# A mixer and expert block: x transposed raw, its norm applied to the transposed tiles

## The reference, cut to what matters

```python
h = x * rsqrt(mean(x*x, axis=-1) + 1e-6) * attn_norm_w        # the first norm
proj = h @ w_in                                                # 1024 -> 2568
qkv, z, beta_logit, a_in, p = split(proj)
qkv = silu(causal_depthwise_conv(qkv, conv_w))                 # 4 taps
o = chunk_gated_delta_rule(q, k, v, g(a_in), sigmoid(beta_logit))
x = x + concat([norm(o) * silu(z), multiscale_pool(p)]) @ w_out
x = x + moe(norm(x), ...)                                      # top 4 of 32, 402 MB of weights
return norm(x)
```

## Time and profile before

| | us |
|---|---|
| three runs | 1407.25, 1410.95, 1411.27 |
| median | 1410.95 |
| the profiled execution, its own time | 1406.2 |
| its span in the trace | 1404.5 |
| TensorE busy in the span | 1280.6 |
| ScalarE, VectorE, GpSimd busy | 293.3, 497.9, 159.2 |

### The profile page before, as it was taken

How to read it: one execution, slowest core, us unless ns; L and a number is a source line. 1 busy time by engine, 2 the same in 40 slices (tenths; PEclk the granted TensorE clock), 3 DMA queues, 4 the chain that set the end, 5 groups by cost and what they waited for, 6 DMA issues and landing times.

```text
span 1404.5 us, 53101 instructions
## 1 busy us (share of the span) xinstructions
PE 1280.6 (91%) x22067; PEld 754.5 (54%) x22067; DVE 497.9 (35%) x1614; ACT 293.3 (21%) x504; POOL 159.2 (11%) x256
## 2 busy tenths in 40 slices
PE   5999999993799999999999999999999999988860
PEld 3456655442455555555555656555555565555430
DVE  4453023215333333333333333333333333332227
ACT  4432212204111112112211121111211111211102
POOL 3100240007010010101100010101101010100000
PEclk9999999995899999999999999999999999999995
DMA  6222132308289999999999999999999999999957
GB/s 207 78 60 62 32 120 76 132 18 335 105 335 416 408 415 402 416 410 418 402 414 403 399 416 400 416 408 417 405 410 411 404 417 399 418 419 417 417 204 295
DMA packets 94582, 447.32 MB, mean 318 GB/s; under 512 B 10973, under 2 KB 22706, under 8 KB 61194
## 3 DMA queue, kind: packets, MB, share of 16 engines
q1 hardware_dynamic: 90778, 437.34, 77.4%
q0 software_dynamic: 3696, 8.40, 1.6%
HBM read 432.52 MB, written 14.88 MB: 319 GB/s over the span
## 4 chain that ended last, share of the span: by engine, by line
PE 59%; DMA 34%; DVE 4%; issue 1%; SPq 0%; ACT 0%; DVEq 0%; POOLq 0%; ACTq 0%
PE ps L1634 22%; DMA ring<-in_w_gate_up_dram 20%; DMA ring<-in_w_down_dram 13%; PE ps L1239 10%; PE ps L1655 10%; PE ps L1259 4%; PE ps L1596 4%; PE ps L1306 2%; DVE ring L1200 1%; PE ps L1627 1%; PE ps L1394 1%; PE ps L1393 1%; PE ps L1646 1%; DMA ring<-pair_rows_dram 1%; PE ps L1299 1%
## 5 line engine op out<-in xcount | busy, mean ns | idle before, releaser
L1634 PE MATMUL ps<-ring,cat 128*32 128x256 f32 x9856 | 553.6, 382 | 14.5 <-DMA ring<-in_w_gate_up_dram 14.5
L1634 PEld LDWEIGHTS ps<-ring,cat 128*32 128x32 f32 x9856 | 306.4, 111 | 233.0 <-DMA ring<-in_w_gate_up_dram 19.2
L1655 PE MATMUL ps<-ring,cat 128*32 128x256 f32 x4928 | 282.7, 379 | 5.8 <-DMA ring<-in_w_down_dram 5.3
L1655 PEld LDWEIGHTS ps<-ring,cat 128*32 128x32 f32 x4928 | 146.0, 110 | 113.6 <-DMA ring<-in_w_down_dram 11.5
L1239 PE MATMUL ps<-hbuf,ring 128*128 128x512 f32 x320 | 145.9, 601 | 0.0
L761 ACT ACTIVATE cat<-cat 128x128 f32<-128x128 f32 x154 | 47.7, 310 | 449.3 <-DVE cat L1181 449.3
L551 POOL DMA_INDIRECT pair_rows_dram<-cat,rowi x77 | 76.9, 999 | 525.3 <-ACT cat L765 525.3
L1165 DVE TENSOR_REDUCE wslot<-ps 128x2 f32<-128x6 f32 x77 | 12.7, 165 | 313.5 <-ACT cat L765 313.0
L765 ACT ACTIVATE cat<-ps,wslot 128x256 f32<-128x256 f32 x77 | 36.5, 474 | 370.7 <-PE ps L1655 370.7
L1596 PE MATMUL ps<-hbuf,cat 128*32 128x256 bf16 x2496 | 108.7, 274 | 4.1 <-DVE cat L1148 4.1
L1181 DVE TENSOR_SCALAR cat<-ps 128x128 f32<-128x128 f32 x154 | 44.9, 292 | 169.6 <-PE ps L1634 168.1
(11 more groups left out here) (305 smaller groups left out, 834.9 us busy)
## 6 DMA issues: line engine op xcount, KB each, us to landing
ring<-in_w_gate_up_dram SPq DMA_DIRECT2D x256, 1024.0 KB, 10.0
ring<-in_w_down_dram SPq DMA_DIRECT2D x128, 1024.0 KB, 10.0
ring<-in_w_in_dram SPq DMA_DIRECT2D x10, 1024.0 KB, 6.0
ring<-pair_rows_dram SPq DMA_DIRECT2D x4, 2048.0 KB, 14.4
ring<-in_w_out_dram SPq DMA_DIRECT2D x1, 4096.0 KB, 13.0
ring<-in_x_dram SPq DMA_DIRECT2D x4, 512.0 KB, 4.9
x_rows_dram<-ring SPq DMA_DIRECT2D x1, 2048.0 KB, 17.6
ring<-x_rows_dram SPq DMA_DIRECT2D x4, 512.0 KB, 6.7
```

The lines of the kernel that those rows point to most:

```text
L1634: last = mm(ps[SLOTS * q:SLOTS * (q + 1), gu_bank(half), 0:2 * P].rearrange("p (s j i) -> p s j i", s=2, j=4), xgT[:, SLOTS * u:SLOTS * (u ...
L1655: last = mm(ps[SLOTS * q:SLOTS * (q + 1), 1, 0:QD], actT[:, c // 4, SLOTS * (c % 4):SLOTS * (c % 4 + 1)], w[:, i, q * QD:(q + 1) * QD], st ...
```

## The change

1. SP no longer issues the parameters. ScalarE issues them as its first four instructions; the four loads of convolution taps are one.
2. ScalarE then takes a root of a constant, and behind each block's square that block's root; each counts `std_ok`.
3. TensorE transposes x itself, as each block lands: tiles 0 to 6 into banks 0 to 6. The parameters' transpose into bank 7 stands behind the second block.
4. For each block VectorE inverts the roots and multiplies the identity by them (`xdiag`). TensorE multiplies it by ones: bank 7 then holds in every partition the row of the 512 tokens' factors. Tile 7 follows into bank 2 when ScalarE has evicted tile 2.
5. VectorE evicts tiles 0 and 1 and ScalarE the other six, with the norm's weight; VectorE then multiplies each of the eight in place by bank 7. project(0) waits for each tile by itself (`ht_ok`).
6. VectorE builds only the first two of the masks ahead of this; two follow ahead of `ba_part`'s copy, two and `icnt` behind conv(0).
7. TensorE's order is project(0), `four_chunks`, project(1), the small products, project(2).

```diff
--- before.py
+++ after.py
@@ -121,7 +121,7 @@
         hT = hbuf[:, :].rearrange("p (k t) -> p k t", k=KD)
         cat = sb("cat", [P, KD * T])
         catT = cat[:, :].rearrange("p (k t) -> p k t", k=KD)
-        xn = cat[:, :].rearrange("p (b d) -> p b d", b=TB)
+        xdiag = cat[:, 0:TB * P].rearrange("p (b i) -> p b i", b=TB)
         DX = cat[:, 0:1024].rearrange("p (c f) -> p c f", c=NC)
         TRk = DX
         TR = cat[:, 1024:2048].rearrange("p (c f) -> p c f", c=NC)
@@ -228,8 +228,8 @@
         y_in = [sem(f"y_in{i}") for i in range(TB)]
         iota_ok, const_ok, lvl_ok, pool_step, pool_mix, bias_ok = [sem(n) for n in (
             "iota_ok", "const_ok", "lvl_ok", "pool_step", "pool_mix", "bias_ok")]
-        std_ok, xn_ok, pcol_ps, pcol_ok, xt_ps, ht_even, ht_odd = [sem(n) for n in (
-            "std_ok", "xn_ok", "pcol_ps", "pcol_ok", "xt_ps", "ht_even", "ht_odd")]
+        std_ok, xdiag_ok, pcol_ps, pcol_ok, xt_ps, ht_ok, hraw_ok, hraw2_ok, rrow_ps = [sem(n) for n in (
+            "std_ok", "xdiag_ok", "pcol_ps", "pcol_ok", "xt_ps", "ht_ok", "hraw_ok", "hraw2_ok", "rrow_ps")]
         proj_ps, tap_ok, conv_ok, silu_ok, ba_ps, dve_step = [sem(n) for n in (
             "proj_ps", "tap_ok", "conv_ok", "silu_ok", "ba_ps", "dve_step")]
         gin_ok, gexp_in, gln_in, g_ok, gcum_ps, gcs_ok, gex_ok, spread_ok = [sem(n) for n in (
@@ -315,17 +315,8 @@
 
         @block.sync
         def _(sp):
-            def param(row, n, src):
-                sp.dma_start(prow[row:row + n, :], src).then_inc(par_in, 16)
             for b in range(TB):
                 sp.dma_start(xs[:, b, :], x[0, b * P:(b + 1) * P, :]).then_inc(x_in[b], 16)
-            param(NANW, KD, attn_norm_w.rearrange("l (k p) -> (l k) p", p=P))
-            for j in range(CONV):
-                param(NCV + NQKV * j, NQKV, conv_w[0, j:j + 1, :].rearrange("l (k p) -> (l k) p", p=P))
-            param(NDN, 1, dn_norm_w)
-            param(NPS, 4, pool_scale.rearrange("l (k p) -> (l k) p", p=P))
             w_in_v = w_in[0].rearrange("(k p) c -> p k c", p=P)
             pieces = (H * P, H * P + 256, 0, 256, 2 * H * P, 2 * H * P + 256, C_P, C_P + 256, C_Z, C_Z + 256)
 
@@ -561,15 +552,23 @@
             def row(v):
                 return v.rearrange("p a t -> p (a t)")
 
+            def param(row, n, src):
+                act.dma_start(prow[row:row + n, :], src).then_inc(par_in, 16)
+            param(NANW, KD, attn_norm_w.rearrange("l (k p) -> (l k) p", p=P))
+            param(NCV, CONV * NQKV, conv_w[0].rearrange("j (k p) -> (j k) p", p=P))
+            param(NDN, 1, dn_norm_w)
+            param(NPS, 4, pool_scale.rearrange("l (k p) -> (l k) p", p=P))
+            act.wait_ge(const_ok, 2)
+            link(A(sm[:, 8:9], epsc[:, 0:1], ACT.Sqrt))
             for b in range(TB):
                 act.wait_ge(x_in[b], 16)
                 link(A(junk, xs[:, b, :], ACT.Square, accum_out=sm[:, b:b + 1]))
-            act.wait_ge(const_ok, 2)
-            A(sm[:, 4:8], sm[:, 0:4], ACT.Sqrt, scale=1.0 / D, bias=epsc[:, 0:1]).then_inc(std_ok, 1)
+                A(sm[:, 4 + b:5 + b], sm[:, b:b + 1], ACT.Sqrt, scale=1.0 / D, bias=epsc[:, 0:1]).then_inc(std_ok, 1)
             act.wait_ge(pcol_ok, 1)
-            for k in range(0, KD, 2):
+            for k in range(2, KD):
                 act.wait_ge(xt_ps, k + 1)
-                A(hT[:, k, :], bank(k), ACT.Copy, scale=pcol[:, NANW + k:NANW + k + 1]).then_inc(ht_even, 1)
+                A(hT[:, k, :], bank(k if k < KD - 1 else 2), ACT.Copy, scale=pcol[:, NANW + k:NANW + k + 1]).then_inc(hraw_ok, 1)
             def tap(m):
                 n = tap_of(m)
                 act.wait_ge(proj_ps, m + 1)
@@ -798,23 +797,35 @@
             link(V.tensor_tensor(lvl[:, 0, :], lvl[:, 0, :], above, ALU.mult))
             link(V.scalar_tensor_tensor(out=lvl[:, 0, :], in0=lvl[:, 0, :], scalar=-1.0, in1=identC,
                                         op0=ALU.mult, op1=ALU.subtract))
-            for s in range(1, LEVELS + 1):
+            def level_mask(s):
                 link(V.tensor_scalar(row_i, spare_i, s, None, ALU.logical_shift_right))
                 link(V.tensor_scalar(lvl[:, s, :], row_i, 1, None, ALU.is_equal))
                 link(V.tensor_tensor(lvl[:, s, :], lvl[:, s, :], below, ALU.mult))
                 link(V.tensor_tensor(lvl[:, s, :], lvl[:, s, :], identC, ALU.add))
-            link(V.tensor_scalar(icnt[:, :], iotaf[:, 0:PAD], 1.0, None, ALU.add))
-            step(V.reciprocal(icnt[:, :], icnt[:, :]), lvl_ok, 1)
+            level_mask(1)
+            def rstd_diagonal(b):
+                dve.wait_ge(const_ok, 3)
+                dve.wait_ge(std_ok, b + 1)
+                link(V.reciprocal(sm[:, 8 + b:9 + b], sm[:, 4 + b:5 + b]))
+                V.tensor_scalar(xdiag[:, b, :], ident, sm[:, 8 + b:9 + b], None, ALU.mult).then_inc(xdiag_ok, 1)
+            rstd_diagonal(0)
+            rstd_diagonal(1)
             dve.wait_ge(pcol_ps, 1)
             step(V.tensor_copy(pcol[:, :], ps[:, 7, 0:61]), pcol_ok, 1)
-            dve.wait_ge(std_ok, 1)
-            link(V.reciprocal(sm[:, 8:12], sm[:, 4:8]))
-            for b in range(TB):
-                V.tensor_scalar(xn[:, b, :], xs[:, b, :], sm[:, 8 + b:9 + b], None, ALU.mult).then_inc(xn_ok, 1)
-            for k in range(1, KD, 2):
+            rstd_diagonal(2)
+            for k in range(2):
                 dve.wait_ge(xt_ps, k + 1)
-                V.tensor_scalar(hT[:, k, :], bank(k), pcol[:, NANW + k:NANW + k + 1], None, ALU.mult).then_inc(ht_odd, 1)
+                step(V.tensor_scalar(hT[:, k, :], bank(k), pcol[:, NANW + k:NANW + k + 1], None, ALU.mult), hraw2_ok, k + 1)
+            rstd_diagonal(3)
+            dve.wait_ge(rrow_ps, 1)
+            for k in range(KD):
+                if k >= 2:
+                    dve.wait_ge(hraw_ok, k - 1)
+                V.tensor_tensor(hT[:, k, :], hT[:, k, :], bank(7), ALU.mult).then_inc(ht_ok, 1)
 
             def conv(m):
 
@@ -833,9 +844,15 @@
             for hh in range(2):
                 r = slice(CH * hh, CH * (hh + 1))
                 link(V.tensor_copy(bch[r], bcr[r, 0:2 * H].rearrange("p (k a b) -> p k a b", k=2, a=2)[:, :, :, hh]))
+            level_mask(2)
+            level_mask(3)
             dve.wait_ge(part_ps, 1)
             V.tensor_copy(ba_part, bank(6)).then_inc(part_ok, 1)
             conv(0)
+            level_mask(4)
+            level_mask(5)
+            link(V.tensor_scalar(icnt[:, :], iotaf[:, 0:PAD], 1.0, None, ALU.add))
+            step(V.reciprocal(icnt[:, :], icnt[:, :]), lvl_ok, 1)
 
             dve.wait_ge(ba_ps, 1)
             ba = ps[:, 7, 0:4 * NCH].rearrange("p (n k a) -> p n k a", n=NCH, k=2)
@@ -1213,17 +1230,30 @@
         @block.tensor
         def _(pe):
             mm, tr = nc.tensor.matmul, nc.tensor.transpose
+            def x_transposed(b, k, to):
+                return tr(bank(to)[:, b * P:(b + 1) * P], xs[:, b, k * P:(k + 1) * P], ident)
+            pe.wait_ge(const_ok, 3)
+            for b in range(TB):
+                pe.wait_ge(x_in[b], 16)
+                for k in range(KD - 1):
+                    last = x_transposed(b, k, k)
+                    if b == TB - 1:
+                        last.then_inc(xt_ps, 1)
+                if b == 1:
+                    pe.wait_ge(par_in, 16 * 4)
+                    tr(ps[:, 7, 0:61], prow[:, :], ident[0:61, 0:61]).then_inc(pcol_ps, 1)
             pe.wait_ge(const_ok, 6)
-            pe.wait_ge(par_in, 16 * (3 + CONV))
-            tr(ps[:, 7, 0:61], prow[:, :], ident[0:61, 0:61]).then_inc(pcol_ps, 1)
             pe.wait_ge(pcol_ok, 1)
-            pe.wait_ge(xn_ok, TB)
-            for k in range(KD):
-                for b in range(TB):
-                    last = tr(bank(k)[:, b * P:(b + 1) * P], xn[:, b, k * P:(k + 1) * P], ident)
-                last.then_inc(xt_ps, 1)
-            pe.wait_ge(ht_even, KD // 2)
-            pe.wait_ge(ht_odd, KD // 2)
+            for b in range(TB):
+                pe.wait_ge(xdiag_ok, b + 1)
+                last = mm(bank(7)[:, b * P:(b + 1) * P], ones, xdiag[:, b, :], start=True, stop=True)
+            last.then_inc(rrow_ps, 1)
+            pe.wait_ge(hraw_ok, 1)
+            for b in range(TB):
+                last = x_transposed(b, KD - 1, 2)
+            last.then_inc(xt_ps, 1)
 
             def project(m, lo=0, hi=KD):
 
@@ -1236,6 +1266,8 @@
                     elif m >= NQKV + 2:
                         pe.wait_ge(silu_ok, m - 1)
                 for k in range(lo, hi):
+                    if m == 0:
+                        pe.wait_ge(ht_ok, k + 1)
                     last = mm(bank(m % 2), win[:, piece % 3, k, m % 2 * P:(m % 2 + 1) * P], hT[:, k, :], start=k == 0,
                               stop=k == KD - 1)
                 if hi == KD:
@@ -1431,9 +1463,10 @@
+            project(0)
             pe.wait_ge(wba_in, 16)
             four_chunks(bank(6), wba, hT, part_ps)
-            project(0)
```

(2 more changed lines are left out.)

## The result

| | before | changed |
|---|---|---|
| median beside the prediction (4 runs each), us | 1410.54 | 1400.08 |
| second comparison (17 and 6 runs), us | 1408.69 | 1399.19 |
| ratio of the first, with its 95% interval | | 0.9932 (0.9911 to 0.9953) |
| ratio of the second | | 0.9935 (0.992 to 0.995) |
| profiled execution: its time, its span | 1406.2, 1404.5 | 1399.2, 1397.4 |

The change makes the kernel faster, by 0.7% in both comparisons (0.68% and 0.65%). The profiled execution took 1399.2, where 1398.7 was forecast for it. In the trace the gain is 6.9 us at the start of `project(2)` and 7.1 at the end of the span, where 7.5 was forecast for both.

A forecast was written before the change was run, and what follows sets the result against it. TensorE bounds the kernel once continuously busy, so the head's gain counts: project(2) at 30.1 instead of 37.6 us, 7.5 earlier. From the median, 1410.95 - 7.5 = 1403.4 us; range 1400.5 to 1409.

The forecast's parts named there:

- What bounds it, and that the gain passes on: TensorE is continuously busy from the projections on, so an earlier start of project(2) shortens the whole time by as much.
- ScalarE's head: Issues end at 2.3 us, 0.6 of cover before x; square-and-root cycle 1.41, fourth root ends at 10.25, winning 1.0.
- Transposes: TensorE before the roots: only transposes behind x's last block are on the path; tile 0 out at about 9.7 us.
- VectorE: Fourth diagonal 0.25 us, row of roots at 12.3, tile 0 multiplied by 13.05, then one tile each 0.69.
- Weights and parameters: First piece of w_in lands at 12.6 us, needed at 13.05, cover 0.5; parameters land at 6.0, no delay.
- The work moved behind: VectorE's masks, copies and gates behind the products stay covered: gates ready at 31.0 us, nothing late.
- (a): Rival: TensorE runs project(0) at its lower clock, costing 1.75 to 3.5 us, total 1405.2 to 1406.9; chance 0.24.
- (b): Rival: parameters land only at 9.7 in the new queue, tile 0 comes 2.1 us later, total 1405.5; chance 0.11.
- (c): Rival: the first piece of w_in arrives late, at 13.6 to 14 us, total 1404 to 1404.4; chance 0.08.
- (d): Rival: ScalarE exchanges its table between each square and root, cycle 4.0 us, total 1412.4; chance 0.03.
- (e): Rival: the head shortens but the end doesn't, as the expert-weight stream ends by itself, total 1411; chance 0.03.
- the sum: project(0) starts at 13.1 instead of 22.57 us, project(2) at 30.1 instead of 37.6: 7.5 us earlier.

The follow-up runs named there:

- order_back: Changed kernel with TensorE's order of before: four_chunks first, behind all eight tiles, then project(0); median 1405.73 us of 12 runs, 0.998 of the kernel before.
- diagonal_first: Changed kernel with VectorE's fourth diagonal between the evictions of tile 0 and tile 1; median 1398.71 us of 6 runs, 0.9943 of the kernel before.
- w_held: Changed kernel with SP waiting for x's third block before it issues the first piece of w_in; 1397.96 us, one run.
- masks_front: Changed kernel with all level masks and icnt ahead of the diagonals again; 1404.56 us, one run.
- params_sp: Changed kernel with the four parameter loads issued by SP, behind x and ahead of w_in; 1403.25 us, one run.
- order_back_filled: order_back with 40 spare transposes of x into bank 0 while VectorE multiplies, output the same; 1404.92 us, one run.

## Why the prediction was right or wrong

**What bounds it, and that the gain passes on:** right. The end follows the head in the profiled pair (6.9 and 7.1) and in the timed order_back, 5.8 at the head and 6.5 in the medians.

**ScalarE's head:** right. The issues ended at 2.40 (2.3 forecast), conv_w as one issue took 0.33, the low bound, and 0.74 us of cover was left. Where x was there, the cycle of square and root was 1.37 to 1.39 (1.41). The fourth root ended at 11.02 instead of 10.25, because the third block of x landed at 8.16 instead of before 7.12 and the fourth could be squared only at 9.57.

**Transposes:** right in kind; tile 0 came out at 10.22 instead of 9.75. In the changed kernel's two traces x's arrival bounds it: in the first over the third root and VectorE's third diagonal, which ended when tile 0 was there, in the second over the fourth block at 9.48 and three transposes. But x is not the only way to be late. I assumed that TensorE goes over to the faster spacing on the way. It did in order_back, and didn't in diagonal_first, where x was as early (third square at 7.44):

```profile
8.11 1.87 PE L1235 MATMUL ps<-ring 128*128 128x128 f32 x14
```

```profile
8.10 2.99 PE L1236 MATMUL ps<-ring 128*128 128x128 f32 x14
```

Tile 0 came at 9.59 in order_back and at 10.11 in diagonal_first. In the changed kernel's first trace the same fourteen took 2.81 us, so there too the spacing stayed slow. My estimate from the prediction's own figures is that this alone kept tile 0 until 8.22 + 8 x 0.206 + 0.35 = 10.2, even if the fourth block had been earlier.

**VectorE:** the diagonal took 0.29, the upper bound, where I took 0.25. The eight products took 4.87 us, 0.61 each, where the form of L1048 had 0.69; since TensorE needs 0.88 per tile this gave nothing. The product began at 12.86 (12.35 forecast) and project(0) at 13.69 (13.1): 0.5 us of the 0.6 is x and tile 0, the rest the 0.14 between product and matmul, which I left out.

**Weights and parameters:** right. The piece landed at 2.7 + 9.8 = 12.5 (12.6), and the parameters were there at 7.93, when TensorE came to them. The cover was 1.1 us, from 12.5 to the 13.56 at which tile 0 was multiplied, and not the 0.5 forecast, since the tile came later; w_held spent it.

**The work moved behind:** right. The masks ended at 28.6 (27.8), the gates at 31.7 (31.0), and from 13.69 on the chain has no gap before 44.68. Nothing became late.

**The rivals.** (a), the cold projection, did not happen in the changed kernel: its first projection took 7.11. It was no idle fear: masks_front paid it (1.4 us) and order_back, too (2.4 us, as the filling gave back). Its price was set too low for the case that it named last: 3.5 us is what 7 us at half speed cost, but all of project(0) at half speed would cost its whole 7.06. In the changed kernel the gaps ahead of the projection are 0.6 and 0.4 us, in its second trace 1.0 and 0.4, in masks_front 1.5, 1.5 and 0.4; that their length is what decides was not tried by itself. (b) didn't happen, and by params_sp would have cost about 0.6 and not 2.1. (c) didn't happen. (d), the exchanged table, is refuted by the timeline of ScalarE: no load among the roots. (e) is refuted by the 7.1 at the end.

**The size, and the low end of the range.** The term of the sum that was mis-sized is the kernel before's own head: I took 37.6 from one execution, and two more had 38.8 and 38.3. With the mean of the three the heads differ by 38.2 - 30.7 = 7.5, by luck the number forecast, since the new head was 0.6 later than I had it. The median that the gain is taken from was thin, too: 1410.95 of three runs, where the 17 runs of the second comparison had 1408.69. With that the forecast would be 1401.2, against 1399.19 measured there. It doesn't explain the first comparison, in which the kernel before had 1410.54.

By the medians the gain was 10.5 in the first comparison, 9.5 in the second and 7.8 for the version with the earlier head; the intervals, 6.6 to 12.6, 7.0 to 11.3 and 5.1 to 11.0, hold 7.5. I gave the range 2 us for the runs' variation, though its low end lies 2.9 below the forecast; the parts behind the head alone vary by 4 between traces. No mechanism found explains the 0.4 below that end, and this variation is enough for it; that it is the cause is not shown. What part of the medians' surplus over 7.5 is real stays open.

**Open:** x's third block landed at 7.0, 7.3 and 7.5 in the three traces with the parameters on SP and w_in issued late, and, of the ten with the parameters on ScalarE, by 7.5 in four, at 7.7 in w_held and at 7.9 to 8.2 in five, though nearly all of these have the same list of loads. In params_sp it was 7.9. So either an early issue of w_in or the second queue may cost x 0.8 us in some executions, or it is chance; the samples don't decide.

## What to carry to other kernels

Where a scale per token stands between a load and a transpose, transpose the raw data as it lands and bring the scale in behind it as a row: the statistics and the transposes then run side by side, and only the last block's remain on the path. Let the first long product take the tiles one by one as they are multiplied: here that order is worth 5.8 us of the head (2.4 of them through the clock), 6.5 by the medians. Price such a head from several traces, since its parts (arrival of a load, spacing of the first transposes) move by 1 us each between executions. And look at TensorE's gaps ahead of the first long run of matmuls: work that fills them kept the clock (4.64 of 4.80 us busy in order_back_filled), small work between gaps of 1.5 us did not (masks_front).

## What was not expected of the hardware

- Gaps need not be long to cost the clock: two of 1.5 us, with 1.0 us of small products between and 0.9 us of work behind, were followed by a granted clock of 0.57 over 3.4 us (masks_front), while in the changed kernel gaps of 0.6 and 0.4 us, and in its second trace of 1.0 and 0.4, left it at 1.00. The Trainium skill (TensorE: Matmul & The Clock Gate, "The HAM clock gate") has the rule that activity releases the throttle; the 40 spare transposes agree, with 2.4 us.
- The granted clock reads 1.00 in the first microseconds whatever the transposes' spacing: in the kernel before it was 0.206 and then 0.13, and the fourteen above took 1.87 us in order_back and 2.99 in diagonal_first, with a granted clock of 1.00 in all. In the head of a program the spacing has to be read beside it. What the slower spacing is no run here shows.
- A table load of 1.28 us disappeared wholly behind the arrival of data when one cheap root was issued first. The squares, the roots and the copies behind them then ran with that one load (at 2.43), where the kernel before had one at 0.79 for the squares and one at 9.64 for the root.
